# Three of eight conditioning chunks of the third K group go from TensorE to VectorE

## The chip, the cores and the metric

The kernel runs on one core of a Trainium2 chip. The metric is the device time of one launch in microseconds (us). TensorE (PE in the profile) multiplies, VectorE (DVE) and ScalarE (ACT) do elementwise work, GpSimd (POOL) small pieces, and SyncE (SP) issues nearly all loads.

## The reference

Two layers of a decoder mixer on 256 tokens of width 2048. What the kernel has to compute, cut to what matters:

```
mod = silu(c) @ w_ada + b_ada                # c is one row of 2048; w_ada is 2048 x 6144
shift, scale, gate = split(mod, 3)
h = rmsnorm(x, norm_pre) * (1 + scale) + shift
z = h @ w_in                                 # 2048 x 14336, in 7 kinds of column blocks
y_conv = gb * causal_conv3(gcin * u, conv_w) * silu(g_c)
y_ret = groupnorm(retention(rope(q), rope(k), v)) * silu(g_r)
x = x + gate * rmsnorm(concat(y_conv, y_ret) @ w_out, norm_post)
```

Everything is float32. The product silu(c) @ w_ada is a vector times a matrix: each weight is used once. It is called the conditioning here.

## The kernel before

**The big product.** The weights w_in come in chunks, one after the other, and a chunk has a number n, here called step n. SyncE loads chunk n into one of four buffers of the tile `stage`. ScalarE rounds it (line 636, tile `w_hi`), VectorE takes the rest (line 849, `low`, tile `w_lo`; this is called lo(n) below), and TensorE multiplies the rows of h by both (lines 1327 to 1329): 12 products for half a chunk (two K tiles, two token tiles, three products each), 24 for a whole one. Results gather in two PSUM tiles Z in turn, so step n needs that the result of step n-2 has been taken out.

**Why there are K groups.** In layer 0 the first products can start only when scale and shift are known. So the K dimension is cut into five groups (`FRONT_GROUPS`: 2, 2, 4, 4 and 4 K tiles). For each group there are seven steps, one for each kind of column block: steps 0 to 6 for the first group, 7 to 13 for the second (all of these of half a chunk), then three whole early chunks of another turn (steps 14, 15, 16), then 17 to 23 for the third group, 24 to 30 for the fourth, and so on. The partial results of each step are added on VectorE into the tile `part` (line 1070). VectorE does so for step n-2 in its iteration n, right after lo(n), or between the two halves of lo(n) in a whole chunk. This is called part(n-2) below. TensorE's step n waits for part(n-2).

**The conditioning in the front.** Each K group g needs two blocks of mod: k = 2g (scale) and k = 2g+1 (shift). The third group's are blocks 4 and 5, and h of that group must be ready when step 17 starts. A block is loaded in chunks of 1 MB written (k, kc); blocks 4 and 5 have four chunks each, eight in all. A chunk is turned into partial sums in one of two ways:

- on TensorE: `front_chunk`, line 1366, four matrix products with 32 columns of stationary operand at different column groups, 512 moving columns each. The profile counts each as two instructions;
- on VectorE: `front_rows`, lines 1004 and 1007, four instructions over 128x512, one multiplies and three multiply and add into `acc` or `acc2`; the first chunk of a block that goes this way starts the sum.

After the last TensorE chunk of a block, `front_row` on VectorE moves the sums out of PSUM (line 1019; line 1021 where VectorE has sums of its own to add), `front_sum` on TensorE turns them over partitions (line 1379), and `front_mods` on VectorE reduces them (lines 882 and 885). The tables `FRONT_USE`, `FRONT_ROW`, `FRONT_MOD` say behind which step each of these stands; `FRONT_VECTOR` says which chunks go to VectorE. A group of chunks that TensorE multiplies behind one step is called a visit.

**The loads.** SyncE issues all loads in one fixed order, `LOADS`, and waits at each for its buffer. The conditioning chunks have a ring of four buffers of their own (`front_stage`, three, and `front_last_stage`), the weight chunks another of four. Load i of the first ring waits until chunk i-4 has been used, on TensorE (`s_front`) or on VectorE (`s_fv`). The order around the change is:

```
... w7, (4,0), (4,1), w8, w9, (4,2), (4,3), w10, w11, (5,0), (5,1), w12, w13, w14, (5,2), (5,3),
w15, (6,0), w16, (6,1), w17, (6,2), w18, (6,3), w19, (7,0), (7,1), w20, (7,2), (7,3), w21 ...
```

Load (5,0) waits for the use of (4,0), (5,1) for that of (4,1), (6,0) for that of (5,0), (6,1) for that of (5,1). All weight loads that stand behind such a load wait with it. w7 to w13 are 0.5 MB each, w14 and later ones 1 MB.

Of the kernel before, what the change touches and what calls it, by code (L numbers as in the profile page):

```python
# [108 lines left out]
for c in CH[:FRONT]:  # L109
    if c.g == 0:  # L110
        PART_NO[c.j, c.b] = len(PART_NO) + 1
    else:
# [27 lines left out]
FRONT_BLOCKS = 2 * len(FRONT_GROUPS)  # L140


FRONT_VECTOR = {k: () for k in range(6)}
FRONT_VECTOR.update({6: (1, 3), 7: (1,), 8: (1, 3), 9: (1,)})

# [3 lines left out]

FRONT_USE = {1: ((2, 0), (2, 1)), 3: ((3, 0), (3, 1)), 7: ((4, 0), (4, 1)), 9: ((4, 2), (4, 3)),
             12: ((5, 0), (5, 1)), 14: ((5, 2), (5, 3))}
for n, k in ((17, 6), (24, 8)):
    FRONT_USE[n] = ((k, 0), (k, 2), (k, 1))
    FRONT_USE[n + 2] = ((k + 1, 0), (k, 3))
    FRONT_USE[n + 3] = ((k + 1, 2), (k + 1, 3), (k + 1, 1))


FRONT_ROW = {2: 2, 4: 3, 10: 4, 15: 5, 20: 6, 21: 7, 27: 8, 28: 9}
FRONT_SUM = FRONT_ROW
FRONT_MOD = {3: 2, 5: 3, 11: 4, 16: 5, 21: 6, 22: 7, 28: 8, 29: 9}
FRONT_H = {6: 1, 16: 2, 23: 3, 30: 4}


# [40 lines left out]
def on_vector(k, kc):  # L208
    return kc in FRONT_VECTOR[k]


def front_done(k, kc):

    upto = FRONT_CHUNKS[:FRONT_CHUNKS.index((k, kc)) + 1]
    return sum(on_vector(*c) == on_vector(k, kc) for c in upto)


def front_last(k):

    return max(kc for m, kc in FRONT_CHUNKS if m == k and not on_vector(k, kc))  # L220
# [36 lines left out]
def build(nc, x, c, positions, norm_pre, norm_post, w_ada, b_ada, w_in, conv_w, gn_gain, w_out,  # L257
          consts, decay, out):
    ctx = ExitStack()
    with ctx:  # L260
# [581 lines left out]
        def _(dve):  # L842
# [52 lines left out]
            def h_split(l, g, half, i=None):  # L895
                k, lo = unit_tiles(half), tokens(i)
                tmp = tmp_buf(g)[:, k.start:k.stop, lo]
                k, hi = slice(4 * g + k.start, 4 * g + k.stop), slice(S + lo.start, S + lo.stop)
                unit = UNIT[l, g, half, i]
                if l:  # L900
                    dve.wait_ge(s_tmp, unit + 1)
                    V.tensor_copy(H[:, k, lo], tmp).then_inc(s_hhi, 1)
                dve.wait_ge(s_hhi, unit + 1)
                V.tensor_tensor(H[:, k, hi], tmp, H[:, k, lo].bitcast(F32), ALU.subtract).then_inc(s_h, 1)
# [87 lines left out]
            def front_rows(k, kc):  # L992
# [4 lines left out]
                dve.wait_ge(sem_, value)  # L997
                first = min(FRONT_VECTOR[k])
                if kc == first:
# [12 lines left out]
            def front_row(k):  # L1012

                cols = slice(0, P * FRONT_GROUPS[k // 2][1])
                dve.wait_ge(s_front, front_done(k, front_last(k)))
                if not FRONT_VECTOR[k]:
                    if k > 1:
                        dve.wait_ge(s_sum, k - 1)
                    V.tensor_copy(front_acc(k)[:, cols], A[:, k % 2, cols]).then_inc(s_row, 1)
                else:  # L1020
                    V.tensor_tensor(front_acc(k)[:, cols], A[:, k % 2, cols], front_acc(k)[:, cols], ALU.add)\
                        .then_inc(s_row, 1)

            def front_mods(k):
                mods(k, 0, 1 - k % 2, *FRONT_GROUPS[k // 2], A[:, k % 2, :])
                if k % 2:
                    gains(0, *FRONT_GROUPS[k // 2], k + 1)

            def front_split(g):
                k0, tiles = FRONT_GROUPS[g]  # L1030
                for k in range(k0, k0 + tiles, 2):
                    h_split(0, k // 4, k % 4 // 2)
# [25 lines left out]
            for n, ch in enumerate(CH):  # L1058
# [33 lines left out]
                if n == NEXT + 1:  # L1092
# [6 lines left out]
                    for g in range(2):  # L1099
                        h_split(1, g, None, 1)  # L1100
                if n in FRONT_MOD:
                    front_mods(FRONT_MOD[n])
                if n in FRONT_ROW:
                    front_row(FRONT_ROW[n])
                if n in FRONT_H:
                    front_split(FRONT_H[n])
                for k, kc in FRONT_USE.get(n, ()):
                    if on_vector(k, kc):
# [187 lines left out]
        def _(pe):  # L1296
# [16 lines left out]
            def products(n, h, i):  # L1313

                ch = CH[n]
                z = Z[ch.q % 2]
                for a in (2 * h, 2 * h + 1):
                    k = ch.k0 + a
                    if ch.out:
                        y, k = (YC, k) if k < KT else (YR, k - KT)  # L1320
                    else:
                        y = H
                    hh, hl = y[:, k, i * P:(i + 1) * P], y[:, k, S + i * P:S + (i + 1) * P]
                    hi, lo = w_bufs(n, h)
                    wh, wl = hi[:, a % 2, :], lo[:, a % 2, :]
                    stop = ch.last and a == 2 * ch.halves - 1
                    T.matmul(z[:, i, :], hh, wh, start=ch.first and a == 0, stop=False)  # L1327
                    T.matmul(z[:, i, :], hh, wl, start=False, stop=False)  # L1328
                    ins = T.matmul(z[:, i, :], hl, wh, start=False, stop=stop)  # L1329
                if i == 0 and ch.out and ch.last and h == 1:  # L1330
                    ins.then_inc(s_o0, 1)
                if i == NT - 1:
                    ins.then_inc(s_pe, 1)
# [90 lines left out]
            for n, ch in enumerate(CH):  # L1424
# [11 lines left out]
                if n not in chain(*BY_TILES):  # L1436
                    z_wait(n)
                    for h in range(ch.halves):
# [7 lines left out]
                        for i in range(NT):  # L1446
                            products(n, h, i)
                for k, kc in FRONT_USE.get(n, ()):
                    if not on_vector(k, kc):
# [115 lines left out]
```

## Time and profile before

| | |
|---|---|
| runs of the kernel | 1712.61, 1712.75, 1714.49 us (median 1712.75) |
| the profiled execution | 1712.71 us |
| its span, first to last instruction | 1710.9 us |
| TensorE busy | 1680.5 us, 98% of the span |
| VectorE busy | 1162.7 us, 68% |
| ScalarE busy | 728.1 us, 43% |
| granted TensorE clock, mean | 0.999 |

TensorE's busy time counts overlapping instructions once, and a busy TensorE is not one at its peak. A time at the left of a timeline row is counted from the start of the span. The profiled execution lies within 0.1 us of the median, and its time is the span and 1.8 us around it.

### The profile page before, as it was taken

Reading aid. Unit: us, or ns where it says so; the run is one execution under the profiler, and the core shown is the slowest. Engines: PE = TensorE matmul, PEld = TensorE weight load, DVE = VectorE, ACT = ScalarE, POOL = GpSimd, SP = SyncE. Lnnn points to the kernel's source line nnn. Section 1 sums busy time; section 2 is a strip of 40 time slices with the busy share of each in tenths; the row PEclk is TensorE's granted clock in tenths of the full one; section 3 lists DMA queues with packets and bytes.
Section 4 is the critical chain, followed back from the end, with each engine's and each line's share of the span. In section 5 each row is a group of like instructions: output and inputs, shape, how many; then the busy total and the mean of one; then the engine's idle time right before and its main releaser. Section 6 shows DMA issues by size and latency. Waiting matters only on the chain. (4 is left out here: it accounts for less than half of the span.)

```text
span 1710.9 us, 19029 instructions
## 1 busy us (share of the span) xinstructions
PE 1680.5 (98%) x7747; PEld 1376.5 (80%) x7747; DVE 1162.7 (68%) x1295; ACT 728.1 (43%) x804; POOL 51.3 (3%) x94
## 2 busy tenths in 40 slices
PE   6999999999999999999999999999999999999998
PEld 4667788888888888888888888888888888888886
DVE  2567867888678778787786455546544654578777
ACT  4444444534444443444454444344344344444442
POOL 4000000000000000000000000000000000000000
PEclk9999999999999999999999999999999999999999
DMA  9989865898798789888855666566556756678884
GB/s 341 383 309 331 288 205 177 291 301 279 242 309 290 250 296 304 306 282 286 294 197 175 202 213 197 174 206 216 191 183 208 214 184 190 207 262 300 289 289 177
DMA packets 233655, 429.25 MB, mean 251 GB/s; under 512 B 8664, under 2 KB 50024, under 8 KB 232800
## 3 DMA queue, kind: packets, MB, share of 16 engines
q1 hardware_dynamic: 225888, 408.97, 70.2%
q10 hardware_dynamic: 7680, 19.07, 3.9%
q8 instruction: 61, 1.00, 0.2%
q14 instruction: 26, 0.21, 0.0%
HBM read 417.57 MB, written 2.10 MB: 245 GB/s over the span
## 5 line engine op out<-in xcount | busy, mean ns | idle before, releaser
L849 DVE TENSOR_TENSOR w_lo<-stage,w_hi 128x1024 fp32r<-128x1024 f32 x574 | 697.4, 1223 | 457.6 <-ACT w_hi L636 454.1
L636 ACT CAST w_hi<-stage 128x1024 fp32r<-128x1024 f32 x574 | 601.8, 1052 | 934.3 <-PE Z L1329 798.5
L1327 PE MATMUL Z<-w_hi,H 128*128 128x512 f32 x1784 | 702.4, 394 | 5.1 <-DVE part L1070 3.2
L1329 PE MATMUL Z<-w_hi,H 128*128 128x512 f32 x1784 | 695.0, 390 | 0.0
L1328 PE MATMUL Z<-w_lo,H 128*128 128x512 f32 x1784 | 694.5, 389 | 0.0
L1327 PEld LDWEIGHTS Z<-w_hi,H 128*128 128x128 f32 x1784 | 334.9, 188 | 81.7 <-DVE part L1070 7.6
L1329 PEld LDWEIGHTS Z<-w_hi,H 128*128 128x128 f32 x1784 | 334.8, 188 | 70.8
L1328 PEld LDWEIGHTS Z<-w_lo,H 128*128 128x128 f32 x1784 | 335.1, 188 | 67.8
L870 DVE SCALAR_TENSOR_TENSOR acc<-stage,c_silu,acc 128x512 f32<-128x512 f32 x240 | 180.2, 751 | 6.8
L1327 PE MATMUL Z<-w_hi,YC 128*128 128x512 f32 x256 | 100.1, 391 | 0.0
L1327 PE MATMUL Z<-w_hi,YR 128*128 128x512 f32 x256 | 99.9, 390 | 0.0
L1328 PE MATMUL Z<-w_lo,YC 128*128 128x512 f32 x256 | 99.7, 389 | 0.0
L1328 PE MATMUL Z<-w_lo,YR 128*128 128x512 f32 x256 | 99.6, 389 | 0.0
L1329 PE MATMUL Z<-w_hi,YR 128*128 128x512 f32 x256 | 99.6, 389 | 0.0
L1329 PE MATMUL Z<-w_hi,YC 128*128 128x512 f32 x256 | 99.6, 389 | 0.0
L1329 PEld LDWEIGHTS Z<-w_hi,YC 128*128 128x128 f32 x256 | 48.1, 188 | 10.1
L1329 PEld LDWEIGHTS Z<-w_hi,YR 128*128 128x128 f32 x256 | 48.1, 188 | 10.0
L1327 PEld LDWEIGHTS Z<-w_hi,YR 128*128 128x128 f32 x256 | 48.1, 188 | 9.9
L1328 PEld LDWEIGHTS Z<-w_lo,YR 128*128 128x128 f32 x256 | 48.1, 188 | 9.8
L1327 PEld LDWEIGHTS Z<-w_hi,YC 128*128 128x128 f32 x256 | 48.1, 188 | 9.8
L1328 PEld LDWEIGHTS Z<-w_lo,YC 128*128 128x128 f32 x256 | 48.1, 188 | 9.8
L1267 POOL MEMSET behind<- 1x512 f32 (+1 forms) x16 | 7.8, 516 | 950.5 <-DVE mv L1172 868.5
(167 smaller groups left out, 737.4 us busy)
## 6 DMA issues: line engine op xcount, KB each, us to landing
stage<-in_w_in SPq DMA_DIRECT2D x186, 1024.0 KB, 5.2
stage<-in_w_ada SPq DMA_DIRECT2D x64, 1024.0 KB, 5.4
stage<-in_w_out SPq DMA_DIRECT2D x64, 1024.0 KB, 5.3
stage<-in_w_in SPq DMA_DIRECT2D x74, 512.0 KB, 4.7
front_stage<-in_w_ada SPq DMA_DIRECT2D x24, 1024.0 KB, 11.5
front_last_stage<-in_w_ada SPq DMA_DIRECT2D x8, 1024.0 KB, 12.6
behind<-R ACTq DMA_DIRECT2D x14, 448.0 KB, 3.5
taps<-in_conv_w ACTq DMA_DIRECT2D x18, 256.0 KB, 6.0
```

Of the source, the lines that this page charges most:

```text
L636: N.copy(w_bufs(n, h)[0], stage[:, slot_of(n), 2 * h:2 * h + 2, :]).then_inc(s_hi, 1)
L849: V.tensor_tensor(lo, stage[:, slot_of(n), 2 * h:2 * h + 2, :], hi.bitcast(F32), ALU.subtract)\
L870: ins = V.scalar_tensor_tensor(acc[:, :], w, c_silu[:, k:k + 1], acc[:, :], ALU.mult, ALU.add)
L1267: ins = G.memset(behind_buf(t)[0:n_back, n_back - 1, 0, :], 0.0)
L1327: T.matmul(z[:, i, :], hh, wh, start=ch.first and a == 0, stop=False)
L1328: T.matmul(z[:, i, :], hh, wl, start=False, stop=False)
L1329: ins = T.matmul(z[:, i, :], hl, wh, start=False, stop=stop)
```

## The change

Of blocks 4 and 5, the chunks (4,1), (4,3) and (5,1) are marked for VectorE. The visits of TensorE for these blocks stood behind steps 7, 9, 12 and 14 with two chunks each. Now they stand behind 9 with (4,0) and (4,2), behind 12 with (5,0), and behind 14 with (5,2) and (5,3). VectorE does (4,1) in iteration 8, (4,3) in 10 and (5,1) in 13. The row and the sum of block 4 go from step 10 to 11 and its mods from 11 to 12; those of block 5 stay. The order of the loads stays, and what the loads wait for follows the user of each chunk.

```diff
-FRONT_VECTOR = {k: () for k in range(6)}
-FRONT_VECTOR.update({6: (1, 3), 7: (1,), 8: (1, 3), 9: (1,)})
+FRONT_VECTOR = {k: () for k in range(4)}
+FRONT_VECTOR.update({4: (1, 3), 5: (1,), 6: (1, 3), 7: (1,), 8: (1, 3), 9: (1,)})

-FRONT_USE = {1: ((2, 0), (2, 1)), 3: ((3, 0), (3, 1)), 7: ((4, 0), (4, 1)), 9: ((4, 2), (4, 3)),
-             12: ((5, 0), (5, 1)), 14: ((5, 2), (5, 3))}
+FRONT_USE = {1: ((2, 0), (2, 1)), 3: ((3, 0), (3, 1)), 8: ((4, 1),), 9: ((4, 0), (4, 2)), 10: ((4, 3),),
+             12: ((5, 0),), 13: ((5, 1),), 14: ((5, 2), (5, 3))}

-FRONT_ROW = {2: 2, 4: 3, 10: 4, 15: 5, 20: 6, 21: 7, 27: 8, 28: 9}
+FRONT_ROW = {2: 2, 4: 3, 11: 4, 15: 5, 20: 6, 21: 7, 27: 8, 28: 9}
 FRONT_SUM = FRONT_ROW
-FRONT_MOD = {3: 2, 5: 3, 11: 4, 16: 5, 21: 6, 22: 7, 28: 8, 29: 9}
+FRONT_MOD = {3: 2, 5: 3, 12: 4, 16: 5, 21: 6, 22: 7, 28: 8, 29: 9}
```

VectorE's order before, from lo(7) on. The first row holds lo(7), lo(8) and lo(9); then come part(7), lo(10), part(8), the row of block 4, lo(11), part(9), the mods of block 4, lo(12) and part(10).

```order
L849 TENSOR_TENSOR w_lo<-stage,w_hi 128x1024 [waits w_hi_done] x3
L1070 TENSOR_TENSOR part<-Z,part 128x1024 [waits partial_copied,half_chunks_multiplied]
L849 TENSOR_TENSOR w_lo<-stage,w_hi 128x1024 [waits w_hi_done]
L1070 TENSOR_TENSOR part<-Z,part 128x1024 [waits partial_copied,half_chunks_multiplied]
L1019 COPY acc<-A 128x512 [waits ada_summed,front_chunk_multiplied]
L849 TENSOR_TENSOR w_lo<-stage,w_hi 128x1024 [waits w_hi_done]
L1070 TENSOR_TENSOR part<-Z,part 128x1024 [waits partial_copied,half_chunks_multiplied]
L882 TENSOR_REDUCE c_sum<-A 128x4 [waits ada_summed]
L885 TENSOR_TENSOR mod<-c_sum,prm 128x4 [waits vector_step]
L849 TENSOR_TENSOR w_lo<-stage,w_hi 128x1024 [waits w_hi_done]
L1070 TENSOR_TENSOR part<-Z,part 128x1024 [waits partial_copied,half_chunks_multiplied]
```

VectorE's order of the changed kernel at the same place, from lo(7) and lo(8) in the first row to part(9).

```order
L849 TENSOR_TENSOR w_lo<-stage,w_hi 128x1024 [waits w_hi_done] x2
L1004 TENSOR_SCALAR acc<-front_stage,c_silu 128x512 [waits ada_summed,front_stage_loaded1]
L1007 SCALAR_TENSOR_TENSOR acc<-front_stage,c_silu,acc 128x512 [waits vector_step] x3
L849 TENSOR_TENSOR w_lo<-stage,w_hi 128x1024 [waits vector_step,w_hi_done]
L1070 TENSOR_TENSOR part<-Z,part 128x1024 [waits partial_copied,half_chunks_multiplied]
L849 TENSOR_TENSOR w_lo<-stage,w_hi 128x1024 [waits w_hi_done]
L1070 TENSOR_TENSOR part<-Z,part 128x1024 [waits partial_copied,half_chunks_multiplied]
L1007 SCALAR_TENSOR_TENSOR acc<-front_last_stage,c_silu,acc 128x512 [waits vector_step,front_stage_loaded3]
L1007 SCALAR_TENSOR_TENSOR acc<-front_last_stage,c_silu,acc 128x512 [waits vector_step] x3
L849 TENSOR_TENSOR w_lo<-stage,w_hi 128x1024 [waits vector_step,w_hi_done]
L1070 TENSOR_TENSOR part<-Z,part 128x1024 [waits partial_copied,half_chunks_multiplied]
```

Four instructions, (4,1), now stand between lo(8) and lo(9), and four more, (4,3), between part(8) and lo(11). The row of block 4 has moved behind part(9).

SyncE's order, as a difference, from loads w10 and w11 in the first row over (5,0), (5,1), w12, w13, w14 and (5,2). `front_chunk_multiplied` is the count of chunks used on TensorE, `front_chunk_added` that of chunks used on VectorE, `w_lo_done` that of lo.

```order
 L612 DMA stage<-in_w_in 128x2x512 [waits w_lo_done] x2
-L588 DMA front_stage<-in_w_ada 128x4x512 [waits front_chunk_multiplied] x2
+L588 DMA front_stage<-in_w_ada 128x4x512 [waits front_chunk_multiplied]
+L588 DMA front_stage<-in_w_ada 128x4x512 [waits front_chunk_added]
 L612 DMA stage<-in_w_in 128x2x512 [waits w_lo_done] x2
 L608 DMA stage<-in_w_in 128x4x256 [waits w_lo_done]
 L608 DMA stage<-in_w_in 128x4x256
 L588 DMA front_stage<-in_w_ada 128x4x512 [waits front_chunk_multiplied]
```

No load changes its place; (5,1) now waits for VectorE. (5,0) waits for the same chunk as before, (4,0), and that chunk's place on TensorE has moved from behind step 7 to behind step 9.

## Rows read from the trace of the kernel before

**Rows 1.** Two stretches of the span; columns named in the first row.
```profile
core 0: us, PE busy (x) PEld busy (x) DVE busy (x) ACT busy (x) POOL busy (x), PEclk, DMA share, GB/s
0.00:90.00 90.00, 71.45 (x438) 48.66 (x439) 40.21 (x57) 39.87 (x48) 19.05 (x38) 1.00 1.04 363
...
200.00:1711.00 1511.00, 1502.38 (x6795) 1247.75 (x6793) 1039.55 (x1144) 640.16 (x697) 30.55 (x52) 1.00 0.72 240
```

**Rows 2.** Waits in 50 to 95 us: who for whom, total, times, longest.
```profile
ACT w_hi L636 <- DMA stage<-in_w_in: 24.1, 8, 6.1
DVE w_lo L849 <- ACT w_hi L636: 13.7, 7, 4.5
```

**Rows 3.** TensorE's timeline: start, duration, instruction, idle time before it.
```profile
54.45 0.39 PE L1328 MATMUL Z<-w_lo,H 128*128 128x512 f32 x1
54.67 0.39 PE L1329 MATMUL Z<-w_hi,H 128*128 128x512 f32 x1
54.99 1.92 PE L1366 MATMUL A<-front_stage,c_cols 128*32 128x512 f32 x16
56.85 0.50 PE L1327 MATMUL Z<-w_hi,H 128*128 128x512 f32 x1
...
60.54 0.48 PE L1327 MATMUL Z<-w_hi,H 128*128 128x512 f32 x1
...
63.45 1.06 PE L1366 MATMUL A<-front_stage,c_cols 128*32 128x512 f32 x8
64.33 1.04 PE L1366 MATMUL A<-front_last_stage,c_cols 128*32 128x512 f32 x8
...
73.29 0.50 PE L1327 MATMUL Z<-w_hi,H 128*128 128x512 f32 x1 [1.72 <-DVE part L1070]
...
80.98 0.39 PE L1327 MATMUL Z<-w_hi,H 128*128 128x512 f32 x1
```

**Rows 4.** SyncE's timeline: when it got through with which loads.
```profile
48.89 3.82 SPq L612 DMA_DIRECT2D stage<-in_w_in  x2
56.12 1.23 SPq L588 DMA_DIRECT2D front_stage<-in_w_ada  x2
```

**Rows 5.** ScalarE's timeline, casts of steps 11 and 12.
```profile
63.03 1.05 ACT L636 CAST w_hi<-stage 128x1024 fp32r<-128x1024 f32 x1 [0.30 <-DMA stage<-in_w_in]
69.79 1.05 ACT L636 CAST w_hi<-stage 128x1024 fp32r<-128x1024 f32 x1 [5.71 <-DMA stage<-in_w_in]
```

**Rows 6.** VectorE's timeline around steps 8 to 12.
```profile
54.67 1.23 DVE L849 TENSOR_TENSOR w_lo<-stage,w_hi 128x1024 fp32r<-128x1024 f32 x1 [3.02 <-ACT w_hi L636]
56.52 1.23 DVE L849 TENSOR_TENSOR w_lo<-stage,w_hi 128x1024 fp32r<-128x1024 f32 x1 [0.63 <-ACT w_hi L636]
57.66 1.22 DVE L1070 TENSOR_TENSOR part<-Z,part 128x1024 f32<-128x1024 f32 x1
...
63.90 1.22 DVE L1070 TENSOR_TENSOR part<-Z,part 128x1024 f32<-128x1024 f32 x1
...
72.02 1.22 DVE L1070 TENSOR_TENSOR part<-Z,part 128x1024 f32<-128x1024 f32 x1
```

**Rows 7.** VectorE's timeline: chunks (6,1) and (6,3), the instruction behind (6,1).
```profile
104.59 0.48 DVE L1004 TENSOR_SCALAR acc<-front_stage,c_silu 128x512 f32<-128x512 f32 x1
...
107.58 3.50 DVE L849 TENSOR_TENSOR w_lo<-stage,w_hi 128x1024 fp32r<-128x1024 f32 x3
...
113.26 3.10 DVE L1007 SCALAR_TENSOR_TENSOR acc<-front_last_stage,c_silu,acc 128x512 f32<-128x512 f32 x4
```

**Rows 8.** A slice of 2 us, columns as in rows 1.
```profile
106.00:108.00 2.00, 2.00 (x12) 1.29 (x15) 1.82 (x3) 1.31 (x3) 0.00 (x0) 1.00 0.00 0
```

**Rows 9.** SyncE's timeline: loads (7,0) and (7,1).
```profile
108.87 0.92 SPq L588 DMA_DIRECT2D front_stage<-in_w_ada  x2
```

**Rows 10.** ScalarE's timeline: the cast of step 20.
```profile
119.49 2.01 ACT L636 CAST w_hi<-stage 128x1024 fp32r<-128x1024 f32 x2 [10.59 <-DMA stage<-in_w_in]
```

**Rows 11.** Line 1366 in 14.8 to 15.9 and in 32.6 to 34.5 us: min/median/max ns.
```profile
L1366 PE MATMUL A<-front_stage,c_cols x12: 634/634/637, 14.9 to 15.7; 128*32 128x256 f32 x12
...
L1366 PE MATMUL A<-front_stage,c_cols x32: 379/379/403, 32.6 to 34.2; 128*32 128x256 f32 x32
```

## The prediction

> **What bounds the kernel now.** I read the busy time by stretches first [rows 1]. From 200 us on TensorE is busy 1502.4 of 1511 us: a delay or a gain made earlier is carried to the end and not lost there, since that part works at TensorE's own pace. In the first 90 us TensorE is busy only 71.5 us, and the DMA engines are at a share of 1.04, 363 GB/s: there the loads are the scarce thing. The change lies in 54 to 89 us, in that stretch.
>
> Next the waits of this stretch [rows 2]. ScalarE waits 24.1 us for loads of weights and VectorE 13.7 us for ScalarE; TensorE waits once, 1.7 us, for a part that VectorE adds [rows 3]. The timelines show that this is one chain. The cast of step 12 waits 5.71 us for its load and starts at 69.79 [rows 5]; lo(12) and part(10) follow it, the latter at 72.02 to 73.24 [rows 6]; and step 12 starts on TensorE at 73.29 after 1.72 us of idle time [rows 3]. So step 12 is set by the landing of w12 (69.75) and not by TensorE.
>
> Last, what sets that landing. w11 lands at about 63.0 and w12 at 69.75 [rows 5]. In between came (5,0), (5,1) and w12, 2.5 MB (2.62 million bytes), in 6.75 us, that is 388 GB/s, more than the stretch's mean of 363 [rows 1]. The DMA engines had no gap. SyncE, though, had one: it was through with w11 at 52.71 and issued (5,0) only at 56.12 [rows 4], which is 1.13 us after TensorE began its visit with (4,0) at 54.99 [rows 3]. The queued data hid this wait of 3.4 us; about 7 us of it was left at 56.12.
>
> **The change part by part.** TensorE's work first. From the product at 54.67 to that at 56.85 is 2.18 us, and an ordinary pitch is 0.22 (54.45 to 54.67), so a visit of two chunks costs 1.96 us; the second chunk of it is 0.88 (63.45 to 64.33) and a visit of one so 1.08 [rows 3]. Four visits of two, 7.84 us, become two of two and one of one, 5.00: 2.8 us less. 1.96 of this goes behind step 7, 0.88 behind step 12.
>
> VectorE's work. A chunk that starts a sum takes it from 104.59 to 107.58, 2.99 us, one that goes on 3.10 [rows 7]. So (4,1) and (5,1) cost 2.99 each and (4,3) 3.10, together 9.1 us on VectorE. The moved row and mods of block 4 cost what they did.
>
> Now the chain, in the changed kernel's own times, with durations from the rows above.
>
> (a) Step 8. The visit behind step 7 is gone; lo(8) is done at 54.67 + 1.22 = 55.89, and step 8 starts at about 55.95, 0.9 earlier than 56.85. TensorE gains no more, as lo(8) hangs on its load.
> (b) Step 9. VectorE starts (4,1) at 55.82 and lo(9) only at 58.81 in place of 56.52, so part(7) goes from 59.95 to 61.17 and not from 57.66. Step 9 needs part(7): it starts at 61.2, 0.7 later than 60.54, though TensorE itself would have been there at 59.6.
> (c) The load (5,0). The visit with (4,0) begins 2.91 us after step 9 (60.54 to 63.45 [rows 3]), at 64.1. SyncE goes on 1.13 later, at 65.25 in place of 56.12: 9.1 us later. Behind it on SyncE's queue stand (5,1), w12, w13, w14 and all that follow. All that was queued has landed at 63.0, so the DMA engines run dry.
> (d) Step 10 and 11. lo(10) and part(8) stay (part(8) at 63.90 [rows 6]; they hang on a load issued before); (4,3) takes 65.04 to 68.15, lo(11) 68.2, part(9) 69.3 to 70.5. Step 11 starts at 70.6 in place of 68.55 and is over at about 73.3; the transposes of block 4's sum end at 73.8.
> (e) The landing of w12. The trace before shows one restart of dry engines: no data moved in 106 to 108 [rows 8], (7,0) was issued at 108.87, and w20 landed at 119.48, 10.6 us later [rows 9, 10], with 3 MB ((7,0), (7,1), w20). Ours is 2.5 MB, 0.5 MB less at 388 GB/s is 1.35 us less: 9.25 us. So w12 lands at 74.5, 4.75 later than 69.75. From both sides: if a restart cost nothing, 6.75 us after 65.25, at 72.0; if the smaller amount saved nothing, 10.6 us, at 75.85. I take 74.5, as this row is the nearest.
> (f) Step 12. Cast 74.5 to 75.55, lo(12) 75.6, part(10) 76.75 to 77.95: step 12 starts at 78.0 in place of 73.29, 4.7 later. TensorE idles for about 4.2 us.
> (g) Step 14. VectorE's queue now holds the mods of block 4 (0.8 us), lo(13), part(11), (5,1), lo(14) and part(12), with a pitch of 1.14 for each lo and part: mods 77.9, lo(13) 78.7, part(11) 79.85, (5,1) 81.0, lo(14) 84.0, part(12) 85.15 to 86.37. TensorE, with its visit shorter by 0.88, would be ready for step 14 at 84.8 and waits for part(12) until 86.4. It was 80.98 [rows 3]: 5.4 us later. What was saved on TensorE is thus given back in this step.
> (h) Behind it. The queue is kept fed: (6,0) is issued 1.13 us after the visit behind step 12 starts (80.9), at 82, while loads already issued last until 87. Everything from step 15 on then keeps its distances: the row of block 5, h of the third group, the next dry spell of the loads, which ends when TensorE uses (6,0). The 5.4 us reach the end.
>
> The sum is 1712.71 + 5.4 = 1718.1 us; the profiled execution is 0.04 us from the median. With the two ends of (e) the same chain gives part(12) done at 83.85 and 87.7, so +2.9 and +6.8: 1715.6 to 1719.5.
>
> On the restart the Trainium skill has a rule (DMA: Bandwidth & Descriptors, "Anatomy of one DMA — SWDGE (gpsimd) path"): a fixed 2 us a transfer and then the bytes at 436 GB/s. By it w12 would land 8.0 us behind (5,0), an estimate from the page, and the sum would be +4.2, 1716.9 us. The row, 10.6 us for 3 MB against 9.2 by the rule, says that it is slower, and the row decides.
>
> On the idle time of (f): the granted clock is 1.00 (2.4 GHz) in every stretch read, but the first matmuls at 14.9 us, after idle time, took 634 ns each where the same form took 379 at 32.6 [rows 11]. A like slowdown in step 12 would stretch it by about 1.7, some 2 us at most; step 14 has 1.6 us of wait to cover that, so at most 0.4 is added. The Trainium skill (TensorE: Matmul & The Clock Gate, "Part 1: The HAM clock gate") says that an array left idle falls to half its clock and has to earn it back, a rule that speaks against any new gap on TensorE; here the gap's price would be hidden by (g).
>
> **The rivals.**
> - *The loads are hidden anyway.* If SyncE's later issue of (5,0) did not delay w12 (more data queued than I read), only VectorE's load would be felt: step 12 at 73.85, mods 73.9 (they wait for the sum), lo(13) 74.7, part(11) 75.8, (5,1) 76.95, lo(14) 79.95, part(12) 81.1 to 82.3, so step 14 at 82.35, +1.4: 1714.1 us. For it speaks that 3.4 us of SyncE's wait are hidden now; against it that w11 lands at 63.0, before the new issue at 65.25.
> - *Faster: TensorE's saved time reaches the end.* TensorE is the engine that is busy 98% of the span, and 2.8 us are taken off it. If VectorE's nine added microseconds all fell into its idle time and the loads came with room, it would be 1712.71 - 2.8 = 1709.9. It decides at step 12: that step must start at 71.3 or earlier, 2 us before 73.29. Against it: w12's landing already holds step 12, and nothing in the change makes it land earlier. Even then only the 0.88 behind step 12 would be left.
> - *More is lost.* (6,1) now waits for (5,1) on VectorE, 84.0 in place of 78.1, and w17 stands behind it; a second dry spell like that of (c) would come if the queue emptied before. It would cost a further restart, about 2.5 us (9.25 less 6.75): 1720.6. Against it: loads issued by then last until 87.
>
> **How the numbers follow.** Forecast 1718.1 with a chance of 0.71; loads hidden 0.14; faster 0.05; more lost 0.10. The forecast's own range is 1715.6 to 1719.5. The range has to hold 8 of 10: I take it down to 1713.9, with the hidden loads at 1714.1, and up to 1719.7, which leaves out faster and more lost. About 0.2%, 3.4 us, is what a measurement of this kernel can tell from no change. Faster by that: 0.03. Slower: the forecast but for its lowest part (+2.9 to +3.4) and more lost, 0.79. The same: 0.18.
>
> **What the profile of the changed kernel would show.** (b) step 9 starting behind part(7) at about 61.2. (c) SyncE issuing (5,0) at about 65, and a slice near 64 to 67 with little or no data moved. (e) the cast of step 12 at about 74.5. (f) an idle time of about 4 us on TensorE before step 12, released by VectorE's part. (g) a second wait for part before step 14, at about 86.4. (h) the same gaps from there on, all 5.4 later, and the same busy time of TensorE less 2.8 us. I am wrong if (5,0) is issued before 60, if the cast of step 12 comes before 71, or if the delay at step 15 is not found at 200 us.

## The result and the profile after

The changed kernel takes 1717.73 us (median of 9 runs, 1717.18 to 1718.53) against 1712.77 of the kernel before (9 runs, 1712.35 to 1714.49). The ratio is 1.0028, with a 95% interval of 1.0019 to 1.0037: 5.0 us slower. The forecast was 1718.1 us. The profiled execution took 1717.73 us with a span of 1715.9 us, 5.0 more than before.

The same two stretches as in [rows 1], in the changed kernel:

```profile
core 0: us, PE busy (x) PEld busy (x) DVE busy (x) ACT busy (x) POOL busy (x), PEclk, DMA share, GB/s
0.00:90.00 90.00, 65.61 (x380) 46.03 (x381) 44.81 (x66) 37.52 (x45) 19.13 (x38) 0.96 0.98 338
...
200.00:1716.00 1516.00, 1507.37 (x6817) 1252.12 (x6815) 1042.86 (x1146) 641.88 (x699) 31.20 (x52) 1.00 0.72 240
```

The difference arises before 90 us: TensorE is busy 65.6 us there in place of 71.5, and the loads bring 338 GB/s in place of 363. Between 90 and 200 us some 1.1 us of it is given back (below, at (g) and (h)). Behind 200 us TensorE works as before, with 8.6 us of idle time in both kernels. A new number is the granted clock of 0.96 in the first stretch, which was 1.00.

The waits of 50 to 95 us, as in [rows 2]:

```profile
ACT w_hi L636 <- DMA stage<-in_w_in: 29.8, 8, 11.0
DVE w_lo L849 <- ACT w_hi L636: 10.9, 5, 4.8
PEld Z L1327 <- DVE part L1070: 9.0, 4, 4.5
PE Z L1327 <- DVE part L1070: 7.2, 3, 4.3
```

TensorE now waits three times, 7.2 us in all, for a part; before it was once, 1.7 us. The longest wait for a load is 11.0 us in place of 6.1.

Next SyncE (answering to [rows 4]), ScalarE's casts of steps 11 and 12 ([rows 5]), and the slices of moved data. This execution is some 0.4 us ahead of the one before at step 8 (lo(8) starts at 54.23, there at 54.67), so a difference of two times is good to about that.

```profile
48.47 3.80 SPq L612 DMA_DIRECT2D stage<-in_w_in  x2
64.84 0.92 SPq L588 DMA_DIRECT2D front_stage<-in_w_ada  x2
```

```profile
62.51 1.05 ACT L636 CAST w_hi<-stage 128x1024 fp32r<-128x1024 f32 x1 [0.22 <-DMA stage<-in_w_in]
74.52 1.04 ACT L636 CAST w_hi<-stage 128x1024 fp32r<-128x1024 f32 x1 [10.96 <-DMA stage<-in_w_in]
```

```profile
60.00:62.00 2.00, 1.23 (x5) 1.05 (x6) 0.72 (x1) 0.77 (x1) 0.00 (x0) 1.00 0.37 135
62.00:64.00 2.00, 2.00 (x12) 1.28 (x14) 1.68 (x2) 1.34 (x2) 0.00 (x0) 1.00 0.02 4
64.00:66.00 2.00, 2.00 (x18) 0.65 (x11) 1.97 (x3) 0.00 (x0) 0.00 (x0) 1.00 0.11 10
66.00:68.00 2.00, 2.00 (x10) 1.60 (x9) 1.78 (x4) 0.00 (x0) 0.00 (x0) 1.00 0.89 272
...
76.00:78.00 2.00, 0.00 (x0) 0.00 (x0) 2.00 (x3) 0.94 (x1) 0.00 (x0) 0.53 1.10 356
78.00:80.00 2.00, 1.99 (x5) 1.60 (x6) 1.97 (x4) 1.11 (x2) 0.00 (x0) 0.50 1.05 385
```

SyncE was through with w11 at 52.3 and then waits until 64.8, the DMA engines move nearly nothing from 62 to 66, and the cast of step 12 starts at 74.52. The last two slices show TensorE idle and then at half its clock (1.2 GHz in place of 2.4).

TensorE, answering to [rows 3], and VectorE around the three chunks, answering to [rows 6, 7]:

```profile
60.77 0.50 PE L1327 MATMUL Z<-w_hi,H 128*128 128x512 f32 x1 [1.31 <-DVE part L1070]
...
63.71 1.92 PE L1366 MATMUL A<-front_stage,c_cols 128*32 128x512 f32 x16
...
70.26 0.50 PE L1327 MATMUL Z<-w_hi,H 128*128 128x512 f32 x1 [1.64 <-DVE part L1070]
...
78.02 0.79 PE L1327 MATMUL Z<-w_hi,H 128*128 128x512 f32 x1 [4.29 <-DVE part L1070]
...
83.23 1.07 PE L1366 MATMUL A<-front_stage,c_cols 128*32 128x512 f32 x8
...
87.09 0.39 PE L1327 MATMUL Z<-w_hi,H 128*128 128x512 f32 x1
```

```profile
55.37 0.48 DVE L1004 TENSOR_SCALAR acc<-front_stage,c_silu 128x512 f32<-128x512 f32 x1
...
58.36 1.23 DVE L849 TENSOR_TENSOR w_lo<-stage,w_hi 128x1024 fp32r<-128x1024 f32 x1
59.50 1.22 DVE L1070 TENSOR_TENSOR part<-Z,part 128x1024 f32<-128x1024 f32 x1
...
80.94 0.47 DVE L1004 TENSOR_SCALAR acc<-front_stage,c_silu 128x512 f32<-128x512 f32 x1
...
85.07 1.22 DVE L1070 TENSOR_TENSOR part<-Z,part 128x1024 f32<-128x1024 f32 x1
```

Steps 9, 11 and 12 each start behind a part of VectorE. Step 12 starts at 78.02, where 78.0 was forecast. From its start to its visit it takes 5.21 us, in place of 2.94 (73.29 to 76.23 in the kernel before): the lower clock. part(12) ends at 86.29 and step 14 starts at 87.09, 6.1 later than in [rows 3] and without a wait.

### The profile page after: what moved, and what is told of

It is laid out like the page before. It is cut to its first block and busy times, and to the rows that moved or that the text cites. A ratio compares the mean times of both kernels' runs of the same rounds, so it can differ in the third digit from the quotient of the medians.

```text
span 1715.9 us, 18997 instructions
## 1 busy us (share of the span) xinstructions
PE 1680.7 (98%) x7723; PEld 1377.8 (80%) x7723; DVE 1170.9 (68%) x1307; ACT 727.4 (42%) x804; POOL 52.0 (3%) x94
## 5 line engine op out<-in xcount | busy, mean ns | idle before, releaser
L1327 PE MATMUL Z<-w_hi,H 128*128 128x512 f32 x1784 | 703.6, 394 | 10.5 <-DVE part L1070 7.8
```

## The experiments

Medians in us. The kernel before was run on the same chip between the others ("before"); ratio and 95% interval are against it. A line of a profile below comes from one execution, which need not be the median one; where the two lie apart, the text says so.

| kernel | median | before | ratio | interval |
|---|---|---|---|---|
| early_visit | 1714.86 | 1712.84 | 1.0012 | 1.0003 to 1.0021 |
| late_visit_pe | 1718.84 | 1712.84 | 1.0031 | 1.0018 to 1.0043 |
| late_visit_pe_warm | 1716.83 | 1712.84 | 1.0021 | 1.0012 to 1.0030 |
| loads_first | 1713.71 | 1712.84 | 1.0006 | 0.9997 to 1.0014 |
| after_warm | 1718.93 | 1712.74 | 1.0035 | 1.0023 to 1.0048 |
| before_loads_first | 1711.48 | 1712.74 | 0.9993 | 0.9984 to 1.0001 |
| one_chunk | 1711.97 | 1712.74 | 0.9994 | 0.9985 to 1.0003 |
| best | 1708.11 | 1712.74 | 0.9974 | 0.9964 to 0.9984 |
| loads_first_late51 | 1712.22 | 1712.79 | 0.9994 | 0.9985 to 1.0002 |
| after_warm_late51 | 1716.25 | 1712.79 | 1.0020 | 1.0011 to 1.0029 |

### early_visit: the chunk that SyncE waits for is used early again

```diff
-... 8: ((4, 1),), 9: ((4, 0), (4, 2)), 10: ((4, 3),),
+... 7: ((4, 0),), 8: ((4, 1),), 9: ((4, 2),), 10: ((4, 3),),
```

> The changed kernel with (4,0) multiplied behind step 7 again, in a visit of its own, and (4,2) behind 9; VectorE keeps its three chunks. Theory (the later use of (4,0) holds SyncE and lets the DMA engines run dry): (5,0) is issued near 56, the DMA share stays near 1 from 60 to 70 us, the cast of step 12 comes near 70, step 12 starts near 74 and waits only for VectorE; in all +1.4 us on the kernel before, 1714.1, some 3.6 faster than the changed kernel. Rival (the nine microseconds added on VectorE are what costs): the time stays at that of the changed kernel, +5.0, 1717.7.

1714.86 us: 2.9 faster than the changed kernel, with VectorE's 9.1 us still there. SyncE, ScalarE and TensorE of this kernel:

```profile
56.65 2.02 SPq L588 DMA_DIRECT2D front_stage<-in_w_ada  x2
```

```profile
69.39 1.05 ACT L636 CAST w_hi<-stage 128x1024 fp32r<-128x1024 f32 x1 [5.72 <-DMA stage<-in_w_in]
```

```profile
70.30 0.50 PE L1327 MATMUL Z<-w_hi,H 128*128 128x512 f32 x1 [2.52 <-DVE part L1070]
...
83.88 0.50 PE L1327 MATMUL Z<-w_hi,H 128*128 128x512 f32 x1 [1.83 <-DVE part L1070]
```

(5,0) and the cast of step 12 are where they were before the change, as expected. The profiled execution took 1716.48 us, the longest of the eleven and 1.6 above the median. In it the granted clock was 0.50 from 72 to 74 and from 86 to 88 us, behind the two waits shown. The first of these makes step 11 longer, so the sum of block 4 and its mods come later, and step 14 starts at 83.9, not at 82.4. The one run with a mean granted clock of 0.999 took 1713.24 us, the other ten, at 0.997 to 0.998, took 1714.71 to 1716.48. So the 0.8 us above the expected time are most likely the clock's; that the median run had one such stretch is not shown.

### late_visit_pe: the visit moved, and nothing on VectorE

```diff
-... 7: ((4, 0), (4, 1)), 9: ((4, 2), (4, 3)),
+... 9: ((4, 0), (4, 1), (4, 2), (4, 3)),
```

(on the kernel before)

> The kernel before with one thing moved: (4,0) and (4,1) are multiplied behind step 9 together with (4,2) and (4,3). VectorE has none of the three chunks. Theory: part(7) is not late, so step 9 starts near 59.6, its visit at 62.5, (5,0) is issued at 63.6, w12 lands 9.25 later at 72.9 and step 12 starts near 76.4, 3.2 later than in the kernel before; if the idle time before it (about 4 us) brings the lower clock, step 12 takes 2.3 more, which nothing hides here: +5.5, 1718.3. Without the clock +3.2, 1716.0. Rival (VectorE's work costs): no change from the kernel before, 1712.8.

1718.84 us, 6.0 above the kernel before, without one added instruction on VectorE. The move of the visit alone makes a loss as large as that of the changed kernel and 1.1 us larger. It holds the price of the lower clock too, which the next run takes apart. SyncE and TensorE:

```profile
63.71 1.23 SPq L588 DMA_DIRECT2D front_stage<-in_w_ada  x2
```

```profile
77.75 0.80 PE L1327 MATMUL Z<-w_hi,H 128*128 128x512 f32 x1 [5.37 <-DVE part L1070]
...
82.68 1.92 PE L1366 MATMUL A<-front_stage,c_cols 128*32 128x512 f32 x16
```

(5,0) is issued at the expected time, w12 lands 10.5 us later (cast at 74.26) where 9.25 were expected, so step 12 starts at 77.75 in place of 76.4, and it takes 4.9 us at the lower clock.

### late_visit_pe_warm: what the clock costs in that

```diff
+                    if n == 12:
+                        pe.wait_ge(s_mod, 4)
+                        bridge(A[:, 1, :], 8)
                     z_wait(n)
```

(on late_visit_pe; `bridge` issues the eight multiplications)

> late_visit_pe with eight multiplications that nothing reads put between step 11 and the wait of step 12 (3.6 us on TensorE, into a PSUM bank that is free then). If the lower clock adds to the price of the gap: the granted clock stays 1.00 through 74 to 84 us, step 12 takes 2.9 us in place of 5.2, and the time is 2.3 below that of late_visit_pe, about 1716.0. If the clock has no part in it, the same time as late_visit_pe.

1716.83 us, 2.0 below late_visit_pe. TensorE and a slice:

```profile
76.05 0.50 PE L1327 MATMUL Z<-w_hi,H 128*128 128x512 f32 x1 [0.53 <-DVE part L1070]
79.00 1.92 PE L1366 MATMUL A<-front_stage,c_cols 128*32 128x512 f32 x16
```

```profile
78.00:80.00 2.00, 2.00 (x17) 0.97 (x19) 1.35 (x2) 1.86 (x2) 0.00 (x0) 1.00 1.06 388
```

Step 12 takes 2.95 us in place of 4.93, and the medians lie 2.0 apart: that much of the price of the gap was the clock's. The two profiles differ in more than this. w12 landed 10.5 us behind (5,0) in the one and 9.1 in the other, for which the edit is no reason, and the one with the eight multiplications has a wait later on that the other lacks:

```profile
182.32 0.50 PE L1327 MATMUL Z<-w_hi,H 128*128 128x512 f32 x1 [1.28 <-DVE part L1070]
```

So the visit behind step 12 comes 3.7 us earlier (79.00 against 82.68), and the end of the execution only 2.4.

### loads_first: the weight loads ahead of the load that waits

```diff
-FRONT_LOAD = {2: 2, 4: 2, 7: 2, 9: 2, 11: 2, 14: 2, 15: 1, ...
+FRONT_LOAD = {2: 2, 4: 2, 7: 2, 9: 2, 13: 2, 14: 2, 15: 1, ...
```

(on the changed kernel)

> The changed kernel with loads w12 and w13 ahead of (5,0) and (5,1) in SyncE's order; use of the chunks as in the changed kernel. Theory: w12 is issued at 56 and lands at 64.4, so that step 12 is held by VectorE only and starts near 73.9; the DMA engines are dry for some 1.7 us instead of 4.7, and this is not felt; step 14 waits for VectorE till 82.4: +1.4, 1714.1. Rival (VectorE's work costs): no change from the changed kernel, 1717.7. If the DMA engines' lost time itself is what counts, wherever it falls: +1.7 to +2.5, about 1715.

1713.71 us: 4.0 faster than the changed kernel, by the place of two loads in the order alone. ScalarE's cast of step 12, and step 14 on TensorE:

```profile
64.05 1.05 ACT L636 CAST w_hi<-stage 128x1024 fp32r<-128x1024 f32 x1 [0.29 <-DMA stage<-in_w_in]
```

```profile
82.34 0.50 PE L1327 MATMUL Z<-w_hi,H 128*128 128x512 f32 x1 [1.80 <-DVE part L1070]
```

The DMA engines are dry for about 2 us here too (20 GB/s from 64 to 66), but w12 is already there. Step 14 waits for part(12) until 82.3, as in the first rival of the prediction. The lost DMA time was not felt yet. The profiled execution took 1714.83 us, 1.1 above the median: behind the wait shown the granted clock falls to 0.50 (84 to 86 us), and step 14 takes 7.28 us to its visit where the kernel before takes 5.53. The five runs with a mean granted clock of 0.999 took 1713.14 to 1713.51 us, so this stretch is most likely missing in them.

### after_warm and after_warm_late51: is step 14 held by VectorE?

after_warm is the changed kernel with the same eight multiplications. after_warm_late51 has (5,1) one iteration later as well (lines on after_warm):

```diff
-             12: ((5, 0),), 13: ((5, 1),), 14: ((5, 2), (5, 3))}
+             12: ((5, 0),), 14: ((5, 1), (5, 2), (5, 3))}
```

> The changed kernel with eight multiplications that nothing reads between step 11 and the wait of step 12. The granted clock should stay 1.00 through 76 to 84 us and step 12 take 2.9 us in place of 5.2. Theory: step 14 then waits for part(12), at about 86.3 in place of 87.1, so only about 0.8 comes back: 1716.9. If VectorE did not hold step 14, the whole 2.3 would come back: 1715.4.

> after_warm with (5,1) in iteration 14 of VectorE. In after_warm step 14 started at 86.6 behind a wait of 1.36 us for part(12). Theory: that wait goes, step 14 starts near 85.2, and the granted clock stays 1.00; 1.4 less than after_warm, about 1717.5, of which up to 1.2 can go either way with the landing of w21. If something else holds step 14 the start stays at 86.6.

The steps behaved as expected, the times did not. Step 14 of after_warm, and steps 12 and 14 of after_warm_late51:

```profile
86.59 0.50 PE L1327 MATMUL Z<-w_hi,H 128*128 128x512 f32 x1 [1.36 <-DVE part L1070]
```

```profile
78.86 0.50 PE L1327 MATMUL Z<-w_hi,H 128*128 128x512 f32 x1 [1.20 <-DVE part L1070]
...
85.66 0.39 PE L1327 MATMUL Z<-w_hi,H 128*128 128x512 f32 x1
```

With the clock at 1.00 step 14 waits 1.36 us for VectorE and gains only 0.5 on the changed kernel's 87.09. With (5,1) later it starts 6.8 us behind step 12 (85.66) without a wait, where it was 8.3 in after_warm. So behind the clock stands (5,1). That the clock hides it, so that moving (5,1) alone would gain nothing at step 14, was not run; it is read from the changed kernel, where TensorE arrives at 87.09 and part(12) is done at 86.29.

The times are 1718.93 (five runs) and 1716.25 us. after_warm was expected at 1716.9 and is 1.2 slower than the changed kernel. In its profile the visit behind step 17 is 0.4 us earlier than in the changed kernel (113.47 against 113.87) and the one behind step 24 is 1.1 later (160.74 against 159.65): between them stands a wait of 1.29 us at step 21, with the later landing of w21 (below). after_warm_late51 was expected at 1717.5. Its profiled execution, with the later landing as well, took 1717.75, 1.2 less than after_warm; seven of its eleven runs lie at 1715.7 to 1716.4 and four at 1717.3 to 1717.8.

### loads_first_late51: both causes taken away, the three chunks kept

> loads_first with one thing more: VectorE does (5,1) in iteration 14, behind both halves of lo(14), not in iteration 13. Theory (g) (step 14 waits for part(12), which stands behind (5,1) on VectorE): the wait of 1.8 us before step 14 goes, and with it the lower clock from 82 to 87 us that follows it (1.2 us); step 14 starts near 80.5 and the time falls by some 2.5 to 3, to about 1711. Rival (the saved TensorE time is lost elsewhere): the time stays at 1713.7.

The edit is the last diff, made to loads_first. 1712.22 us, 1.5 less than loads_first and not to be told from the kernel before. Half of the expected gain came. The wait before step 14 is gone, the clock stays at 1.00, and a new wait stands one step on:

```profile
88.97 0.50 PE L1327 MATMUL Z<-w_hi,H 128*128 128x512 f32 x1 [0.91 <-DVE part L1070]
```

The cast of step 15 waited for its load until 85.48, 3.2 us later than in the kernel before; here the dry time is felt. Against the five runs of loads_first at a mean clock of 0.999 the gain is 0.9 to 1.3 us, and the wait of 1.80 less the new one of 0.91 is 0.9.

### before_loads_first, one_chunk and best

before_loads_first is the kernel before with the loads of loads_first. one_chunk is the kernel before with (5,1) on VectorE in iteration 14. best is both, and (6,0) in a visit behind step 16. The diff of best against the kernel before, cut: the loads are those of loads_first, and (6,0) is taken out of the visit behind step 17.

```diff
-FRONT_VECTOR = {k: () for k in range(6)}
-FRONT_VECTOR.update({6: (1, 3), ...
+FRONT_VECTOR = {k: () for k in range(5)}
+FRONT_VECTOR.update({5: (1,), 6: (1, 3), ...
-             12: ((5, 0), (5, 1)), 14: ((5, 2), (5, 3))}
+             12: ((5, 0),), 14: ((5, 1), (5, 2), (5, 3)), 16: ((6, 0),)}
```

> The kernel before with loads w12 and w13 ahead of (5,0) and (5,1). Theory (w12's landing sets step 12): w12 lands near 64.4, step 12 starts without the 1.7 us of idle time, and the gain stays to the end: -1.7, 1711.1. Rival (the DMA engines are full there, so that the time only moves to the next load): no change, 1712.8.

> The kernel before with (5,1) alone on VectorE, behind lo of step 14, where it idles 4.5 us. Theory: TensorE's visit behind step 12 is 0.9 shorter, nothing waits for VectorE and nothing is loaded later: -0.9, 1711.9. Rival (VectorE's added work costs wherever it stands): 0 to +1.

> before_loads_first and one_chunk together, and (6,0) multiplied behind step 16, not 17, so that load (7,0), which waits for it, is issued some 5 us earlier. Theory: -1.7 - 0.9, and up to -1.4 for the waits at steps 20 and 21, less 0.2 for one more visit: 1709.0 (at least 1710.2 if the last part brings nothing). Rival: the gains do not add, as the full DMA engines take them back: 1711 or more.

before_loads_first takes 1711.48 us (1711.1 expected) and one_chunk 1711.97 (1711.9 expected). These are gains of 1.3 and 0.8 us in the medians, each with an interval that reaches 1, so neither is shown by itself. best takes 1708.11 us, 0.9 less than expected, 4.6 less than the kernel before and 9.6 less than the changed one. In best, TensorE at steps 12 and 17, SyncE at (7,0), and a slice of 4 us around that of [rows 8], which showed no data:

```profile
71.75 0.50 PE L1327 MATMUL Z<-w_hi,H 128*128 128x512 f32 x1 [0.48 <-DVE part L1070]
...
98.92 0.47 PE L1327 MATMUL Z<-w_hi,H 128*128 128x512 f32 x1 [0.30 <-DVE w_lo L849]
```

```profile
98.68 6.78 SPq L588 DMA_DIRECT2D front_stage<-in_w_ada  x2
```

```profile
104.00:108.00 4.00, 3.87 (x22) 2.20 (x21) 3.82 (x5) 2.02 (x2) 0.00 (x0) 1.00 0.65 200
```

Step 12 waits 0.48 us in place of 1.72 (0.48 in before_loads_first too). (7,0) goes out at 98.7 in place of 108.9. TensorE's waits before steps 17, 20 and 21, which were 1.28, 0.28 and 1.16 us in the kernel before, are 0.30, 0 and 0. That last edit was not run alone: that it brings the remaining 2.6 us is read from these rows and the sum, not shown by itself.

## Why the prediction was right

**(a) to (d), VectorE and SyncE.** (4,1) takes 2.99 us; step 9 starts at 60.77 (61.2 forecast), (5,0) goes out at 64.84 (65.25), step 11 starts at 70.26 (70.6). Each is 0.3 to 0.4 us early, by the 0.4 us that this execution is ahead.

**(e), the restart of the loads.** w12 lands 9.6 us behind (5,0), 9.25 were forecast; the two ends were 6.75 and 10.6. In late_visit_pe_warm, after_warm, after_warm_late51 and late_visit_pe the same 2.5 MB took 9.1, 9.8, 9.9 and 10.5 us. That the forecast 9.25 comes within 0.4 us is thus in part luck: the same restart differs by 1.4 us from profile to profile. The Trainium skill's rule (DMA: Bandwidth & Descriptors, "Anatomy of one DMA — SWDGE (gpsimd) path") gave an estimate of 8.0 us, which was too few here. That section fits single transfers issued by GpSimd; these are three, issued by SyncE into empty queues.

early_visit and loads_first show the cause: take away SyncE's hold, or let w12 pass ahead of it, and 2.9 and 4.0 of the 5.0 us come back. late_visit_pe shows that the hold, with the lower clock that it brings, makes a loss of this size without any work on VectorE. What loads_first still lies above the kernel before, 0.9 us in the medians with an interval that reaches 1, goes when (5,1) is moved on VectorE (loads_first_late51).

**(f), the clock.** The idle time was forecast at 4.2 us and is 4.29. That step 12 might then run at the lower clock was said too, at a price of some 2 us at most, of which at most 0.4 would be left at step 14; the sum itself held it at nothing. It costs 2.27. TensorE comes to step 14 at 87.09, 0.8 us after part(12) was done (86.29) and 0.7 after the forecast 86.4, so this term was too small. The second wait for a part before step 14, which the prediction named as a sign, is not there for the same reason. The Trainium skill's rule that an idle array falls to half its clock (TensorE: Matmul & The Clock Gate, "Part 1: The HAM clock gate") agrees with this trace, where the granted clock is 0.50 behind the 4.29 us. The price was not wholly hidden.

**(g), (h), the end.** Step 14 is 6.1 late in place of 5.4 (0.4 from the landing of w12, 0.7 from the clock, less the 0.4 by which this execution is ahead). The visit behind step 17 is at 113.87 in place of 107.75, still 6.1. But at the visit behind step 24 only 4.9 is left (159.65 in place of 154.78), and the span ends 5.0 later. Step (h) held that all distances stay, and the prediction called itself wrong if the delay at step 15 was not found at 200 us. By that sign 1.1 us of it failed: step 15 is 6.1 late (94.47 in place of 88.37), the end 5.0. All distances stay but one. The kernel before waits at step 21, and the changed one does not:

```profile
132.33 0.50 PE L1327 MATMUL Z<-w_hi,H 128*128 128x512 f32 x1 [1.16 <-DVE part L1070]
```

ScalarE's casts of steps 21 and 22, before and then after:

```profile
128.84 2.00 ACT L636 CAST w_hi<-stage 128x1024 fp32r<-128x1024 f32 x2 [7.34 <-DMA stage<-in_w_in]
131.55 2.00 ACT L636 CAST w_hi<-stage 128x1024 fp32r<-128x1024 f32 x2 [0.72 <-DMA stage<-in_w_in]
```

```profile
133.71 2.00 ACT L636 CAST w_hi<-stage 128x1024 fp32r<-128x1024 f32 x2 [6.13 <-DMA stage<-in_w_in]
137.67 2.00 ACT L636 CAST w_hi<-stage 128x1024 fp32r<-128x1024 f32 x2 [1.96 <-DMA stage<-in_w_in]
```

w21 lands 9.35 us behind w20 (cast at 119.49 [rows 10]) in the one and 8.13 (125.58 to 133.71) in the other, w22 12.1 in both. So the forecast of 5.4 met 5.0 with two errors that nearly cancel: 0.7 too little at step 14, and 1.2 given back at step 21, of which the prediction knew nothing. That part of the agreement is luck. The mechanism, SyncE held by the later use of (4,0) and w12 landing late for it, is what was forecast.

TensorE's busy time was to fall by 2.8 us and did not (1680.7 in place of 1680.5). The slow step 12 puts 2.3 back; the rest, some 0.7, was not traced.

**The rivals.** "The loads are hidden anyway" did not happen, but loads_first is that case made on purpose: 1713.71, where 1714.1 was worked out for it. "Faster": step 12 would have had to start by 71.3 and started at 78.02. "More is lost": (6,1) went out at 85.32, where 84.0 was forecast, and the visit behind step 17 is no later for it than step 14 (6.1 both).

## What to carry to other kernels

In a fixed queue of loads, the use of a buffer is a date for every load behind the one that waits for it: before a consumer is moved by two steps to save one microsecond, ask how much data is still queued at the new date. A load that has to wait belongs behind those that need not, if they are used first. And work moved to an engine that is 68% busy on average has to be put where that engine idles, not ahead of a result that the busy engine waits for.

## What was not expected of the hardware

- **The clock falls after short waits.** In the profiles the granted clock went to 0.50 (1.2 GHz) in or soon after waits of TensorE of 1.80 us (loads_first), 1.83 and 2.52 (early_visit), 4.29 (changed kernel) and 5.37 (late_visit_pe), and stayed at 1.00 behind 1.72 (kernel before) and 1.81 (one_chunk). In early_visit the products turned slow (0.63 in place of 0.39 us each) at 71.85, some 1.5 us after the work had begun again at 70.30. So the length of the wait alone does not decide it, and runs of one kernel differ: those of loads_first have mean granted clocks of 0.996 to 0.999. What decides it was not tried.
- **A load lands in two ways.** In the profiles w21 lands about 8.1 us behind w20 (changed kernel, early_visit, loads_first, one_chunk, loads_first_late51) or 9.3 to 9.5 (kernel before, late_visit_pe, late_visit_pe_warm, before_loads_first, after_warm, after_warm_late51), and in the second case TensorE waits 1.1 to 1.3 us at step 21. The runs of one kernel show steps of about this size: one_chunk's lie at 1710.4 to 1710.8, 1712.0 to 1712.2 and 1713.4 to 1713.5; the last three have a mean granted clock of 0.998, as the longest of the kernel before (1714.1 and more) have, so that step may be the clock's. None of the runs of the kernel before is under 1712.3, so the earlier landing may never occur in it. A second place is step 28: w28 lands 9.5 us behind w27 in late_visit_pe_warm (casts at 169.37 and 178.83) and 8.1 in late_visit_pe (173.10 and 181.24), and only the first has the wait of 1.28 us at 182.32. The two landings make the profiled one_chunk look 2.3 us faster than the kernel before, where the medians say 0.8. What decides it is open: a first guess, the chunks on VectorE, falls with after_warm.
